# Expert pairs: the few-token way put directly behind the branch, the rare ways behind it

## The chip, the cores and the metric

The kernel runs on one core of a Trainium2 chip. The metric is the device time of one execution in microseconds. Before the change the median of three runs is 2189.8 us (2189.2 to 2190.83).

## The reference

256 tokens of width 1024 (float32 throughout) go through two networks one after the other: `first_block`, two layers with four attention branches each, and `second_block`, two layers, the first with differential attention, the second with a recurrent mixer (RWKV-7), each followed by a layer norm, a hierarchical mixture of experts and another layer norm. The change is in the mixture of experts, which is computed twice:

- A router picks for every token one of 4 groups and in it 2 of 8 experts, and gives a gate for each of the two.
- Each of the 32 experts has `w_gu` (1024 x 1024: gate and up, 512 columns each) and `w_down` (512 x 1024). For its tokens it computes `down(silu(gate) * up)`; a token's output is the gated sum over its two experts.
- 512 assignments fall on 32 experts. An expert gets 16 tokens on average, but its count depends on the data, and the kernel must be right for any count.

## The kernel before

The program is written by hand, one instruction stream for each engine, with semaphores between them (`Done` counts an engine's steps; a wait is for a count). It is fully unrolled; the only control flow are the branches spoken of here.

`sync_program` issues the weight DMAs. `experts` streams the expert weights of a stage: 16 pairs of experts, six chunks of 2 MB for each pair (`gu0` to `gu3`, `dn0`, `dn1`), into eight buffers (four of the ring, four lent from the arena). A chunk is issued once TensorE has finished with the chunk that was in its buffer eight chunks before. Nothing else moves much data in these two stages ("first stage" is the mixture of layer 0, "second stage" that of layer 1, at the end of the program).

`moe` of `tensor_program`, `vector_program` and `scalar_program` is the work on a stage. VectorE makes one-hot matrices from the routing (`places`), TensorE gathers the tokens of four experts at a time with them (`next_four` gathers for a later pair), and VectorE writes two flags for each pair: `e.flag` tells whether one of the pair's experts has more than 32 tokens, `e.flag2` whether one has more than 96. Every engine of the three loads the flags of each pair from SBUF (`value_load`) and branches. There are three ways through a pair:

- the few way (up to 32 tokens): both experts at once in column groups of 32, 32 matmuls of 512 columns for gate and up, 4 transposes, the gather for a later pair, 16 matmuls for down, 4 to bring the rows back to their tokens;
- the heavy way (33 to 96): the same for three rounds of 32 tokens, with further tokens gathered and further places turned first;
- the full way (over 96): all 256 tokens densely.

Each matmul and gather written here shows as two MATMUL and two LDWEIGHTS in the trace, being fp32, a transpose as one of each. In the order of the code a pair consists of: load of flag, branch (L910, L911 on TensorE), load of flag2, branch (L912, L913), full way, heavy way (L948 on), few way (L1032 on). So the few way is reached by jumping over the other two, the heavy way by falling through the first branch and jumping over the full way, and from the heavy way's end the code jumps over the few way (this jump is shown at L948). VectorE has its branches at L1882 and L1884, ScalarE at L2455 and L2457. All matmuls are recorded at the lines of their helpers: L410 and L417 (`mm` and `mm_to`) and L423 (`tr`).

What orders the work of a few pair on TensorE: a wait for each chunk's landing (`m.w.landed`), for ScalarE's copy of the products (`s gu`) ahead of the transposes, for VectorE's `s hs` ahead of down, and for ScalarE's `all in` of the next pair ahead of the last four matmuls. Before the first pair TensorE also waits for `first xe` (VectorE) and `0 all in` (ScalarE), two copies out of PSUM. VectorE adds a pair's product to `acc` (L1945, L1948), and behind the last pair comes the layer norm on ScalarE and VectorE.

Of the kernel before, what the change touches and what calls it, by code (L numbers as in the profile page):

```python
# [13 lines left out]
P = 128  # L14
S = 256
D = 1024
# [384 lines left out]
def tensor_program(t, m):  # L401
# [461 lines left out]
    def moe(l):  # L863
# [37 lines left out]
        for pr in range(E // 2):  # L901
# [5 lines left out]

            if pr == 0:
                t.wait_ge(*dve(M + "flags"))
            many = t.value_load(e.flag[0:1, pr:pr + 1], min_val=0, max_val=1)  # L910
            with t.If(many != 0):  # L911
                most = t.value_load(e.flag2[0:1, pr:pr + 1], min_val=0, max_val=1)  # L912
                with t.If(most != 0):  # L913

                    t.wait_ge(*dve(N + "all in"))
                    t.wait_ge(*act(N + "all in"))
                    for w in wg:
                        t.wait_ge(*m.w.landed(w))
                    for a in range(2):
                        bufs = (psum[0], psum[1]) if a else (pg, pt)  # L920
                        lst = [(dst[:, n * 256:(n + 1) * 256], gv[k // 2][:, k % 2, a * D + c * 512 + n * P:a * D + c * 512 + (n + 1) * P],
                                hT[:, k, :], k == 0, k == KT - 1)
                               for c, dst in enumerate(bufs) for n in range(4) for k in range(KT)]
                        if a:
                            mm_to(lst, before + 14, N + "gu3")
                        else:
                            mm(lst, N + "f gu0")
                    t.wait_ge(*dve(N + "f hid0"))
                    next_four(pr, pg, N + "f ")
                    for w in wd:  # L930
                        t.wait_ge(*m.w.landed(w))
                    t.wait_ge(*dve(N + "f hid1"))
                    for a in range(2):
                        h3 = e.hid[a].rearrange("p (k s) -> p k s", k=4)
                        if a:
                            t.wait_ge(*act(N1 + "all in"))
                            t.wait_ge(*dve(N + "f xe"))
                        for i in range(NT):
                            buf = (pg, pt)[i] if a else psum[i]
                            lst = [(buf[:, n * 512:(n + 1) * 512], h3[:, k, i * P:(i + 1) * P],  # L940
                                    dv[k // 2][:, k % 2, a * D + n * 512:a * D + (n + 1) * 512], k == 0, k == 3)
                                   for n in range(2) for k in range(4)]
                            if a and i:
                                mm_to(lst, before + 44, N + "out")
                            else:
                                mm(lst, N + f"f down{a}{i}")
                    t.wait_ge(*dve(N1 + "all in"))
                with t.Else():  # L948
# [80 lines left out]
                            else:  # L1029
                                mm(lst, N + "m back0")  # L1030
                    t.wait_ge(*dve(N + "m xe"))
            with t.Else():  # L1032

                pe.n = before
                xp = e.xe[pr // 2 % 2].rearrange("p (k e n) -> p k e n", k=KT, e=4)
                if pr:
                    t.wait_ge(*act(N0 + "s gu"))
                else:
                    t.wait_ge(*act(N + "all in"))
                if pr == 0:  # L1040
                    t.wait_ge(*dve(M + "first xe"))
                elif pr % 2 == 0:
                    t.wait_ge(*dve(N0 + "s xe"))
                for q in range(4):
                    t.wait_ge(*m.w.landed(wg[q]))
                    mm_to([(pg[64 * a + 32 * c:64 * a + 32 * c + 32, 0:512], xp[:, 2 * q + kk, 2 * (pr % 2) + a, :],
                            gv[q][:, kk, a * D + c * 512:a * D + (c + 1) * 512], q + kk == 0, q == 3 and kk == 1)
                           for kk in range(2) for a in range(2) for c in range(2)], before + (8, 9, 10, 14)[q], N + f"gu{q}")
                t.wait_ge(*dve(N + "all in"))
                t.wait_ge(*act(N + "s gu"))  # L1050
                tr([(psum[0][:, k * P:(k + 1) * P], e.gu[:, k * P:(k + 1) * P], idn) for k in range(4)], N + "s guT")
                next_four(pr, pt, N + "s ")
                t.wait_ge(*dve(N + "s hs"))
                for q in range(2):
                    t.wait_ge(*m.w.landed(wd[q]))
                    mm_to([(psum[0][64 * n + 32 * a:64 * n + 32 * a + 32, 512:1024], e.hs[:, 2 * q + kk, a, :],
                            dv[q][:, kk, a * D + n * 512:a * D + (n + 1) * 512], q + kk == 0, q + kk == 2)
                           for kk in range(2) for n in range(2) for a in range(2)], before + 26 + 6 * q, N + f"dn{q}")
                t.wait_ge(*act(N1 + "all in"))
                ogT = e.ogT[pr // 2 % 2][:, 256 * (pr % 2):256 * (pr % 2) + 256]  # L1060
                for i, buf in enumerate((psum[1], psum[0])):
                    lst = [(buf[:, n * 512:(n + 1) * 512], ogT[64 * n:64 * n + 64, i * P:(i + 1) * P], e.yb[64 * n:64 * n + 64, :],
                            True, True) for n in range(2)]
                    if i:
                        mm_to(lst, before + 44, N + "out")
                    else:
                        mm(lst, N + "s back0")

        ps.restart()
        ps.free = [((dve, M + "experts"), (act, M + "experts"))] * 4  # L1070
# [275 lines left out]
def vector_program(v, m):  # L1346
# [462 lines left out]
    def moe(l):  # L1809
# [35 lines left out]
        def behind_oh():  # L1845
# [2 lines left out]
            red(cnt, p[:, 64:96].rearrange("p (q a) -> p q a", a=2), MAX, M + "count")  # L1848
            ts(cnt2, cnt, 3 * CAP + 0.5, None, ALU.is_gt, None)
            cp(e.flag2, cnt2)  # L1850
            ts(cnt, cnt, CAP + 0.5, None, ALU.is_gt, None)
            cp(e.flag, cnt, M + "flags")
            gates_of(l)

# [21 lines left out]
        for pr in range(E // 2):  # L1876
            N, N1 = M + f"{pr} ", M + f"{pr + 1} "
            before = dve.n
            if pr == 0:
                v.wait_ge(*dve(M + "flags"))  # L1880
            many = v.value_load(e.flag[0:1, pr:pr + 1], min_val=0, max_val=1)
            with v.If(many != 0):  # L1882
                most = v.value_load(e.flag2[0:1, pr:pr + 1], min_val=0, max_val=1)
                with v.If(most != 0):  # L1884
                    for a in range(2):
                        bufs = (psum[0], psum[1]) if a else (pg, pt)
                        v.wait_ge(*act(N + f"f sig{a}"))
                        tt(e.hid[a], e.hid[a], bufs[0], MUL)
                        tt(e.hid[a], e.hid[a], bufs[1], MUL, N + f"f hid{a}")
# [14 lines left out]
                with v.Else():  # L1904
# [27 lines left out]
                    v.wait_ge(*pe(N + "out"))  # L1932
                    after_own()
                    v.tensor_tensor(acc[:, 1, :], acc[:, 1, :], psum[0], ADD).then_inc(*added(1, before, pr))
            with v.Else():
                dve.n = before
                g5 = psum[0][:, 0:512].rearrange("p (k a c n) -> p k a c n", k=4, a=2, c=2)
                v.wait_ge(*act(N + "s sig"))
                tt(e.sg, e.sg, g5[:, :, :, 0], MUL)
                tt(e.hs, e.sg, g5[:, :, :, 1], MUL, N + "s hs")  # L1940
                next_four(pr, pt, N + "s ")
                based(pr)
                v.wait_ge(*pe(N + "s back0"))
                after_own()
                v.tensor_tensor(acc[:, 0, :], acc[:, 0, :], psum[1], ADD).then_inc(*added(0, before, pr))  # L1945
                v.wait_ge(*pe(N + "out"))
                after_own()
                v.tensor_tensor(acc[:, 1, :], acc[:, 1, :], psum[0], ADD).then_inc(*added(1, before, pr))  # L1948
        dve.name(M + "experts")
        wide, shift = e.xe  # L1950
        for i in range(NT):
# [198 lines left out]
def scalar_program(s, m):  # L2150
# [273 lines left out]
    def moe(l):  # L2424
# [24 lines left out]
        for pr in range(E // 2):  # L2449
            N, N1 = M + f"{pr} ", M + f"{pr + 1} "  # L2450
            before = act.n
            if pr == 0:
                s.wait_ge(*dve(M + "flags"))
            many = s.value_load(e.flag[0:1, pr:pr + 1], min_val=0, max_val=1)
            with s.If(many != 0):  # L2455
                most = s.value_load(e.flag2[0:1, pr:pr + 1], min_val=0, max_val=1)
                with s.If(most != 0):  # L2457
                    for a in range(2):
                        bufs = (psum[0], psum[1]) if a else (pg, pt)
                        s.wait_ge(*pe(N + ("gu3" if a else "f gu0")))  # L2460
# [4 lines left out]
                with s.Else():  # L2465
# [17 lines left out]
                    cp(e.yb, pg[:, 0:512], N + "m yb0")  # L2483
                    s.wait_ge(*pe(N + "dn1"))
                    last(e.yb2[1], psum[0][:, 0:512], before + 15, N1 + "all in")
            with s.Else():
                act.n = before
                g5 = psum[0][:, 0:512].rearrange("p (k a c n) -> p k a c n", k=4, a=2, c=2)
                s.wait_ge(*pe(N + "gu3"))
                cp(e.gu, pg[:, 0:512], N + "s gu")  # L2490
                s.wait_ge(*pe(N + "s guT"))
                fn(e.sg, g5[:, :, :, 0], ACT.Sigmoid, N + "s sig")
                next_four(pr, pt, N + "s ")
                s.wait_ge(*pe(N + "dn1"))
                last(e.yb, psum[0][:, 512:1024], before + 15, N1 + "all in")
        act.name(M + "experts")
        for i in range(NT):

# [459 lines left out]
```

## Time and profile before

| | |
|---|---|
| median of three runs | 2189.8 us (2189.2 to 2190.83) |
| the profiled execution: its own time, its span | 2188.98 us, 2187.1 us |
| TensorE matmul / weight load, busy | 1798.6 us (82%) / 1128.6 us (52%) |
| VectorE, ScalarE, GpSimd, busy | 598.5 us (27%), 393.8 us (18%), 36.0 us (2%) |
| DMA | 539.53 MB, mean 247 GB/s |
| the chain of waits that ended last | TensorE 69%, DMA 18%, issue 5%, VectorE 5%, ScalarE 3% |

TensorE is busy for most of the span, but the shares are averages over stages with different limits. "Issue" is time in which an engine waited for nothing that the profile shows. The first mixture lies at about 885 to 1370 us of the span, the second at 1712 us to the end.

### The profile page before, as it was taken

Reading aid. Unit: us, or ns where it says so; the run is one execution under the profiler, and the core shown is the slowest. Engines: PE = TensorE matmul, PEld = TensorE weight load, DVE = VectorE, ACT = ScalarE, POOL = GpSimd, SP = SyncE. Lnnn points to the kernel's source line nnn. Section 1 sums busy time; section 2 is a strip of 40 time slices with the busy share of each in tenths; the row PEclk is TensorE's granted clock in tenths of the full one; section 3 lists DMA queues with packets and bytes.
Section 4 is the critical chain, followed back from the end, with each engine's and each line's share of the span. In section 5 each row is a group of like instructions: output and inputs, shape, how many; then the busy total and the mean of one; then the engine's idle time right before and its main releaser. Section 6 shows DMA issues by size and latency. Waiting matters only on the chain.

```text
span 2187.1 us, 30973 instructions
## 1 busy us (share of the span) xinstructions
PE 1798.6 (82%) x13574; PEld 1128.6 (52%) x13574; DVE 598.5 (27%) x1032; ACT 393.8 (18%) x760; POOL 36.0 (2%) x28
## 2 busy tenths in 40 slices
PE   6999999999999987766666878799987777876664
PEld 4788884879886764322222332575984332322211
DVE  1132312123421145221111211564345221211102
ACT  2333211313301143100000100241222010100001
POOL 0000000000000000000000000001030000000000
PEclk9999999999999998888788899899998798988977
DMA  9322333333243533899999997213004899999995
GB/s 340 97 89 97 135 137 145 141 77 135 77 154 139 207 116 150 370 425 425 425 426 425 425 400 291 77 58 117 4 23 177 365 424 426 422 425 425 425 425 224
DMA packets 51465, 539.53 MB, mean 247 GB/s; under 512 B 7440, under 2 KB 16272, under 8 KB 18224
## 3 DMA queue, kind: packets, MB, share of 16 engines
q1 hardware_dynamic: 49248, 527.06, 59.2%
q0 software_dynamic: 1152, 6.29, 0.8%
q8 instruction: 171, 2.80, 0.5%
q10 hardware_dynamic: 848, 3.00, 0.4%
q14 instruction: 46, 0.38, 0.0%
HBM read 535.28 MB, written 1.05 MB: 245 GB/s over the span
## 4 chain that ended last, share of the span: by engine, by line
PE 69%; DMA 18%; issue 5%; DVE 5%; ACT 3%; DVEq 0%; ACTq 0%
PE ps L410 53%; PE ps L417 13%; DMA arena<-in_moe_w_gu 6%; DMA ring<-in_moe_w_gu 5%; DMA arena<-in_moe_w_down 3%; DMA ring<-in_moe_w_down 3%; PE ps L423 3%; DVE x L1369 1%; ACT arena L2171 1%; DVE arena L1358 1%; ACT hb L2167 1%; DVE mT L1945 1%; DVE mT L1948 0%; ACT arena L2442 0%; ACT arena L2167 0%
## 5 line engine op out<-in xcount | busy, mean ns | idle before, releaser
L410 PE MATMUL ps<-hT,ring 128*128 128x256 f32 (+2 forms) x1888 | 391.1, 372 | 0.0
L410 PEld LDWEIGHTS ps<-hT,ring 128*128 128x128 f32 (+2 forms) x1888 | 330.7, 185 | 52.7 <-issue 3.4
L417 PE MATMUL ps<-arena 128*32 128x512 f32 (+1 forms) x1572 | 240.8, 698 | 102.6 <-issue 67.1
L417 PE MATMUL ps<-ring,arena 128*32 128x512 f32 x1472 | 213.1, 713 | 106.0 <-issue 72.5
L2171 ACT ACTIVATE arena<-ps 128x512 f32<-128x512 f32 (+4 forms) x145 | 94.5, 652 | 895.8 <-PE ps L417 519.3
L410 PE MATMUL ps<-arena 64*64 64x64 f32 (+10 forms) x1944 | 186.5, 322 | 56.3 <-ACT arena L2442 22.2
L1358 DVE TENSOR_TENSOR arena<-arena,ps 128x256 f32<-128x256 f32 (+2 forms) x82 | 46.0, 561 | 551.2 <-ACT arena L2167 464.2
L417 PEld LDWEIGHTS ps<-arena 128*32 128x32 f32 (+1 forms) x1572 | 64.5, 130 | 256.2 <-issue 202.0
L410 PEld LDWEIGHTS ps<-arena 64*64 64x64 f32 (+4 forms) x1944 | 113.8, 159 | 130.8 <-ACT arena L2442 53.4
L417 PEld LDWEIGHTS ps<-ring,arena 128*32 128x32 f32 x1472 | 53.3, 126 | 245.7 <-issue 194.4
L410 PE MATMUL ps<-ring,hT 128*128 128x256 f32 (+4 forms) x576 | 149.4, 418 | 8.7 <-ACT hT L2167 6.9
L410 PE MATMUL ps<-arena,ring 64*64 64x64 f32 (+2 forms) x1120 | 140.3, 300 | 5.9 <-DVE arena L1369 2.8
L410 PE MATMUL ps<-ring,arena 64*64 64x64 f32 (+3 forms) x1328 | 129.0, 312 | 14.1 <-issue 8.3
L410 PEld LDWEIGHTS ps<-arena,ring 64*64 64x64 f32 (+2 forms) x1120 | 122.7, 164 | 21.6 <-DVE arena L1369 3.2
L410 PEld LDWEIGHTS ps<-ring,hT 128*128 128x128 f32 x576 | 99.5, 193 | 51.0 <-issue 28.2
L410 PEld LDWEIGHTS ps<-ring,arena 64*64 64x64 f32 (+3 forms) x1328 | 72.4, 138 | 62.9 <-issue 55.9
L1945 DVE TENSOR_TENSOR mT<-mT,ps 128x1024 f32<-128x1024 f32 x29 | 35.4, 1222 | 172.7 <-PE ps L410 172.7
L423 PEld LDWEIGHTS ps<-tcom,arena 128*128 128x128 f32 (+1 forms) x370 | 41.9, 142 | 61.9 <-issue 57.6
L423 PE MATMUL ps<-tcom,arena 128*128 128x128 f32 (+1 forms) x370 | 53.4, 280 | 24.5 <-ACT arena L2171 24.5
L410 PE MATMUL ps<-ring,mT 64*64 64x64 f32 (+1 forms) x704 | 73.3, 287 | 0.2 <-issue 0.2
L2167 ACT ACT_TABLE_LOAD x50 | 64.2, 1283 | 44.6 <-DVE small L1363 18.9
L410 PE MATMUL ps<-arena,x 128*128 128x128 f32 x512 | 69.8, 296 | 1.5 <-DVE arena L1358 1.5
(173 smaller groups left out, 1259.2 us busy)
## 6 DMA issues: line engine op xcount, KB each, us to landing
ring<-in_moe_w_gu SPq DMA_DIRECT2D x64, 2048.0 KB, 28.7
arena<-in_moe_w_gu SPq DMA_DIRECT2D x64, 2048.0 KB, 31.2
arena<-in_moe_w_down SPq DMA_DIRECT2D x32, 2048.0 KB, 33.4
ring<-in_moe_w_down SPq DMA_DIRECT2D x32, 2048.0 KB, 33.4
ring<-in_w_merge SPq DMA_DIRECT2D x16, 2048.0 KB, 7.6
ring<-in_w_in SPq DMA_DIRECT2D x10, 2048.0 KB, 7.5
ring<-in_attn_w_qkv SPq DMA_DIRECT2D x6, 2048.0 KB, 7.3
ring<-in_rw_w_rkv SPq DMA_DIRECT2D x6, 2048.0 KB, 7.7
```

Source lines behind the costliest of these rows:

```text
L410: i = t.matmul(o, l, r, start=first, stop=last, skip_group_check=True)
L417: i = t.matmul(o, l, r, start=first, stop=last, skip_group_check=True)
L423: i = t.transpose(o, a, e)
L1358: v.tensor_tensor(o, a, b, op).then_inc(*dve.one(name))
L1369: v.scalar_tensor_tensor(out=o, in0=a, scalar=s, in1=b, op0=op0, op1=op1).then_inc(*dve.one(name))
L1945: v.tensor_tensor(acc[:, 0, :], acc[:, 0, :], psum[1], ADD).then_inc(*added(0, before, pr))
L2167: s.activation(o, a, f, **k).then_inc(*act.one(name))
L2171: s.activation(o, a, ACT.Copy).then_inc(*act.one(name))
```

## The change

The first flag is turned around (`few` is set where no expert of the pair has more than 32 tokens), and the two bodies of the first branch change places, on all three engines: the few way is now directly behind the branch, and the full and the heavy way, with the second flag's load and branch, are in its else part. The body of each way is the same as before. Setting the step count back (`pe.n = before`) is bookkeeping of the program that writes the code and gives no instruction. On TensorE:

```diff
-            many = t.value_load(e.flag[0:1, pr:pr + 1], min_val=0, max_val=1)
-            with t.If(many != 0):
+            few = t.value_load(e.flag[0:1, pr:pr + 1], min_val=0, max_val=1)
+            with t.If(few != 0):
+
+                pe.n = before
+                xp = e.xe[pr // 2 % 2].rearrange("p (k e n) -> p k e n", k=KT, e=4)
...
+                    if i:
+                        mm_to(lst, before + 44, N + "out")
+                    else:
+                        mm(lst, N + "s back0")
+            with t.Else():
                 most = t.value_load(e.flag2[0:1, pr:pr + 1], min_val=0, max_val=1)
                 with t.If(most != 0):
+                    pe.n = before
...
-            with t.Else():
-
-                pe.n = before
-                xp = e.xe[pr // 2 % 2].rearrange("p (k e n) -> p k e n", k=KT, e=4)
...
```

and where VectorE makes the flag:

```diff
-            ts(cnt, cnt, CAP + 0.5, None, ALU.is_gt, None)
+            ts(cnt, cnt, CAP + 0.5, None, ALU.is_lt, None)
             cp(e.flag, cnt, M + "flags")
```

VectorE's and ScalarE's streams change in the same manner. In the order of the code a pair now consists of: load of flag, branch, few way, jump over the rest, load of flag2, branch, full way, heavy way.

## Rows read from the trace of the kernel before

**Rows 1.** The page: GB/s in 40 slices; packets, MB, share of TensorE's instruction queue.

```profile
GB/s 340 97 89 97 135 137 145 141 77 135 77 154 139 207 116 150 370 425 425 425 426 425 425 400 291 77 58 117 4 23 177 365 424 426 422 425 425 425 425 224
...
q8 instruction: 171, 2.80, 0.5%
```

**Rows 2.** The chain of waits: start us, us, what.

```profile
1169.14 34.13 DMA arena<-in_moe_w_gu
...
2125.45 38.13 DMA arena<-in_moe_w_down
```

**Rows 3.** Windows: us, busy of PE, PEld, DVE, ACT, POOL; PEclk, DMA share, GB/s.

```profile
888.00:892.00 4.00, 4.00 (x28) 1.16 (x32) 0.00 (x0) 0.00 (x0) 0.00 (x0) 0.68 0.01 4
...
1716.00:1720.00 4.00, 4.00 (x24) 1.12 (x20) 0.00 (x0) 0.00 (x0) 0.00 (x0) 0.50 0.29 66
```

**Rows 4.** TensorE's branch lines: duration ns min/median/max, starts (L948: first stage alone).

```profile
L910 PEldq TENSOR_LOAD <-arena x32: 297/302/494, 881.9 to 2137.5; - x32
...
L911 PEldq COMPARE_BRANCH  x32: 80/6210/7052, 882.7 to 2138.2; - x32
...
L913 PEldq COMPARE_BRANCH  x3: 6128/6227/6317, 1217.5 to 1836.1; - x3
...
L948 PEldq COMPARE_BRANCH  x2: 313/313/313, 1267.4 to 1340.6; - x2
```

**Rows 5.** The first branch on VectorE and on ScalarE, the same columns.

```profile
L1882 DVEq COMPARE_BRANCH  x32: 50/56/72, 885.9 to 2140.7; - x32
...
L2455 ACTq COMPARE_BRANCH  x32: 40/45/55, 883.9 to 2137.4; - x32
```

**Rows 6.** TensorE in few pairs: timeline (start, us, instructions, idle before), and one branch.

```profile
911.35 5.15 PE L417 MATMUL ps<-arena 128*32 128x512 f32 x32 [5.30 <-issue]
...
928.89 1.02 PE L417 MATMUL ps<-arena 64*128 64x512 f32 x4
...
L911 PEldq COMPARE_BRANCH  x1: 6333/6333/6333, 952.0 to 952.0; - x1
...
958.52 5.43 PE L417 MATMUL ps<-ring,arena 128*32 128x512 f32 x27 [5.18 <-issue]
...
964.26 0.63 PE L417 MATMUL ps<-ring,arena 128*32 128x512 f32 x3 [0.31 <-issue]
```

**Rows 7.** Timeline at the first pair of each stage.

```profile
883.10 0.60 ACT L2171 ACTIVATE arena<-ps 128x512 f32<-128x512 f32 x1 [1.62 <-PE ps L423]
...
887.91 8.36 PE L417 MATMUL ps<-ring,arena 128*32 128x512 f32 x64 [4.84 <-issue]
...
1710.87 0.60 ACT L2171 ACTIVATE arena<-ps 128x512 f32<-128x512 f32 x1 [2.77 <-PE ps L423]
...
1714.69 1.94 PE L417 MATMUL ps<-ring,arena 128*32 128x512 f32 x8 [3.86 <-issue]
```

**Rows 8.** TensorE's timeline in pairs 12, 13 and 15 of the first stage.

```profile
1223.82 5.06 PE L410 MATMUL ps<-ring,arena 128*32 128x512 f32 x23 [5.77 <-issue]
...
1275.44 5.34 PE L417 MATMUL ps<-arena 128*32 128x512 f32 x32 [3.62 <-issue]
...
1348.82 6.56 PE L417 MATMUL ps<-ring,arena 128*32 128x512 f32 x32 [3.81 <-issue]
1355.20 3.62 PE L417 MATMUL ps<-arena 128*32 128x512 f32 x32
...
1361.64 5.28 PE L417 MATMUL ps<-arena 128*32 128x512 f32 x32 [1.39 <-DVE arena L1358]
...
1377.70 1.94 PE L423 MATMUL ps<-tcom,x 128*128 128x128 f32 x8 [8.01 <-DVE x L1369]
```

**Rows 9.** Chunks issued at 1895.2, 1718.4 and 891.2 us: time to landing.

```profile
DMA to landing us min/median/max: 11.6/11.6/11.6
...
DMA to landing us min/median/max: 7.2/7.2/7.2
...
DMA to landing us min/median/max: 7.9/7.9/7.9
```

More of the change, by code:

```diff
@@ L1031, in moe @@
                     t.wait_ge(*dve(N + "m xe"))
-            with t.Else():
-                pe.n = before
-                xp = e.xe[pr // 2 % 2].rearrange("p (k e n) -> p k e n", k=KT, e=4)
[L1036 to L1067, printed above, removed]
         ps.restart()
@@ L1880, in moe @@
                 v.wait_ge(*dve(M + "flags"))
-            many = v.value_load(e.flag[0:1, pr:pr + 1], min_val=0, max_val=1)
-            with v.If(many != 0):
+            few = v.value_load(e.flag[0:1, pr:pr + 1], min_val=0, max_val=1)
+            with v.If(few != 0):
+                dve.n = before
+                g5 = psum[0][:, 0:512].rearrange("p (k a c n) -> p k a c n", k=4, a=2, c=2)
+                v.wait_ge(*act(N + "s sig"))
+                tt(e.sg, e.sg, g5[:, :, :, 0], MUL)
+                tt(e.hs, e.sg, g5[:, :, :, 1], MUL, N + "s hs")
+                next_four(pr, pt, N + "s ")
+                based(pr)
+                v.wait_ge(*pe(N + "s back0"))
+                after_own()
+                v.tensor_tensor(acc[:, 0, :], acc[:, 0, :], psum[1], ADD).then_inc(*added(0, before, pr))
+                v.wait_ge(*pe(N + "out"))
+                after_own()
+                v.tensor_tensor(acc[:, 1, :], acc[:, 1, :], psum[0], ADD).then_inc(*added(1, before, pr))
+            with v.Else():
                 most = v.value_load(e.flag2[0:1, pr:pr + 1], min_val=0, max_val=1)
                 with v.If(most != 0):
+                    dve.n = before
                     for a in range(2):
@@ L1934, in moe @@
                     v.tensor_tensor(acc[:, 1, :], acc[:, 1, :], psum[0], ADD).then_inc(*added(1, before, pr))
[L1935 to L1948, printed above, removed]
         dve.name(M + "experts")
@@ L2453, in moe @@
                 s.wait_ge(*dve(M + "flags"))
-            many = s.value_load(e.flag[0:1, pr:pr + 1], min_val=0, max_val=1)
-            with s.If(many != 0):
+            few = s.value_load(e.flag[0:1, pr:pr + 1], min_val=0, max_val=1)
+            with s.If(few != 0):
+                act.n = before
+                g5 = psum[0][:, 0:512].rearrange("p (k a c n) -> p k a c n", k=4, a=2, c=2)
+                s.wait_ge(*pe(N + "gu3"))
+                cp(e.gu, pg[:, 0:512], N + "s gu")
+                s.wait_ge(*pe(N + "s guT"))
+                fn(e.sg, g5[:, :, :, 0], ACT.Sigmoid, N + "s sig")
+                next_four(pr, pt, N + "s ")
+                s.wait_ge(*pe(N + "dn1"))
+                last(e.yb, psum[0][:, 512:1024], before + 15, N1 + "all in")
+            with s.Else():
                 most = s.value_load(e.flag2[0:1, pr:pr + 1], min_val=0, max_val=1)
                 with s.If(most != 0):
+                    act.n = before
                     for a in range(2):
@@ L2485, in moe @@
                     last(e.yb2[1], psum[0][:, 0:512], before + 15, N1 + "all in")
[L2486 to L2495, printed above, removed]
         act.name(M + "experts")
```

28 lines of the change are left out of this document (added).

## The prediction

> **What bounds the kernel now.** I read the page first. Its row of GB/s [rows 1] has two long runs of about 425: the two expert stages, in which 192 chunks of 2 MB of expert weights come in. A pair's six chunks of 2 MB take 6 × 4.9 = 29.5 us there, and a pair that takes the way for few tokens keeps TensorE for 23.9 us: a gap of 5.3 us before 911.35 and work from there to 929.9 [rows 6], so over most of a stage TensorE has 5 to 6 us of slack per pair. The chain of waits says where that holds [rows 2]: the second stage ends on the landing of a last chunk; the first leaves the DMAs at 1203.3 and goes by TensorE to its end at 1369.7, 8.0 us before TensorE's next matmul [rows 8]. The reason is in the lines of the branches [rows 4]: of 32 pairs three take the heavy way (the branch for the full way is always taken, so none needs that). By their times they are pairs 12 and 14 of the first stage and pair 5 of the second. A heavy pair holds TensorE for some 50 us against 29.5 us of stream, so with two among the last four pairs the stage ends on TensorE. The stream is stopped in one more place, each stage's start: all eight buffers are full until the first pair frees one, and 888 to 892 and 1716 to 1720 us show 4 and 66 GB/s [rows 3].
>
> Then the branches. The flag takes 0.30 us to load [rows 4] and, with two register steps, 0.65 us until its branch. The branch behind it takes 0.08 us where it is not taken and some 6.2 us where it is taken to the few code, over the full and the heavy code [rows 4]. It is no slow instruction: the heavy pairs' branch over the full code alone takes 6.2 us too, while the jump from the end of the heavy code over the few code takes 0.31 us. Counted in the code, with two matmuls and two weight loads in the trace for each fp32 matmul written, the few code is some 250 instructions, the heavy one 750, the full one 680.
>
> How much is there behind a landing? The branch at 952.0 ends at 958.35; 27 matmuls follow, and the next waits until 964.26 [rows 6], 5.9 us after the landing. I read this as one block present and the following one usable 5.9 us later.
>
> **The change, part by part.** It swaps which way falls through. Nothing is computed otherwise, and no DMA is moved.
>
> 1. *Few to few (24 of 30 passages).* Before: load 0.65, taken branch 6.2. After: a jump of 6.2 at the end of the few code, over heavy and full code, then load 0.65 and 0.08. The same work, in another order, in the same gap of 5.3 us [rows 6]: 0, and where the stream bounds there are 6 us of cover besides. ScalarE and VectorE take their branches in 0.04 to 0.07 us, over the same distance [rows 5]: 0.
>
> 2. *The first pair of a stage.* Nothing is jumped over. TensorE must still wait for the copies of ScalarE, over at 883.70 and 1711.47 [rows 7]; with 0.15 us behind them its matmuls start at 883.85 instead of 887.91 and 1711.65 instead of 1714.69: -4.1 and -3.0. Besides, the granted clock was 0.68 and 0.50 of full speed behind these gaps [rows 3], so at the lower level, 1.2 GHz, for most or all of the stretch. With a gap of 0.8 us I expect the higher level, 2.4 GHz, to stay. The first 64 matmuls of the first stage took 8.4 us [rows 7] against twice 3.6, 32 of a later pair 5.3 against 3.6 [rows 8]: the first buffer comes free 1.1 to 1.7 us sooner, and I take 1.4. The stream, idle here, moves with it: -5.4 and -4.4. The last pair's new jump lies beside the layer norm, in TensorE's 8.0 us idle [rows 8] in the first stage and behind its last work in the second: 0; without that cover it would cost its 6.3.
>
> 3. *Few to heavy (3).* Before, from load to first matmul 7.7 us in pair 12 (the load starts at 1216.1, as the last matmuls of pair 11 do, the heavy ones at 1223.8, [rows 8]). After: jump 6.3, load 0.65, a taken branch over the few code, whose target is in the block that comes 5.9 us after the landing (so 5.25 more), load 0.65, branch over the full code 6.9 (behind the block just asked for, as the longest of the row that reaches 7.05), 0.1. Sum 19.8: +12.1. The lowest bound for the middle branch is the 0.31 us of the jump over the same code [rows 4], the highest a wholly new fetch, 6.9.
>
> The Trainium skill, "Runtime: NRT & Kernel Launch", Instruction fetch mechanics, gives TensorE 128 KiB of code memory, 2048 instructions, and also says that prefetch is sequential over a two-page window. By the first figure a branch over 250 instructions would always land in loaded code; by the second it waits as in my sum. The jumps of some 1,430 and 680 instructions that take 6.2 us speak for the second.
>
> 4. *Heavy to few (3).* The heavy code is now the last and falls through. Before, TensorE idled 3.6 to 3.8 us here (its queue still ran while the sequencer fetched) and restarted at the lower level: the first 32 matmuls took 5.3 us in pair 13 and 6.56 in pair 15, against 3.6 at the higher [rows 8]. After: -3.6 and -1.6 at pair 13; -3.8 and -2.9 at pair 15, and -1.6 for its last 32 (5.28 us), if the clock stays up.
>
> *First stage.* Pair 12 still begins on a landed chunk, so it moves with the stream, and from there all is TensorE: -5.4 + 12.1 - 3.6 - 1.6 + 12.1 - 3.8 - 2.9 - 1.6 = +5.3.
>
> *Second stage.* Its end moves with the stream: -4.4, plus what heavy pair 5 takes from it. TensorE comes out of pair 5 later by 12.1 - 3.7 = 8.4. The tightest chunk is issued at 1895.2 and lands 11.6 us later, where an idle stream needs 7.2 to 7.9 [rows 9]: 4.1 of slack. The rest, 4.3, the stream loses. Net -0.1.
>
> Sum +5.2. The profiled execution took 2188.98 us (span 2187.1, 1.9 around it), so 2194.2 by its own time; it stands 0.8 below the median of 2189.8, which gives the forecast, 2195.0. Its own range is 2190 to 2200: 1.65 us twice for the middle branch at its upper bound, 1 to 2 us for what a heavy pair's start costs at the lower clock after a longer gap, and as much the other way. A measurement tells 0.2% from no change here, 4.4 us; this case lies just above that.
>
> **Rivals.** *The middle branch is cheap* (faster). If TensorE's memory reaches 250 instructions past a landing at once, few to heavy costs 6.3 + 0.65 + 0.31 + 0.65 + 6.9 + 0.1 = 14.9, +7.2 instead of +12.1. First stage -4.5; in the second, 12.1 becomes 7.2 and the stream's slack holds it, -4.4. That is 8.9 less than 2189.8: 2180.9. It decides once the wait in that branch is under about 3 us. For it: 0.31 us for the same distance. Against: there the engine had long read ahead, and the stall at 964.26. The page's first figure (the Trainium skill, as above) would give this case.
>
> *The clock does not come back* (slower). Nothing in rows shows what is granted to these stretches when the gap before them goes. Without the gains of 1.4 + 1.4 + 1.6 + 2.9 + 1.6: +8.9 on the forecast, 2203.9; a tenth of it already puts the time over the bound of 0.2%. For it: pair 15 is slow even in its last 32 matmuls, far from the gap. Against: matmuls behind gaps of 0.8 us keep their 3.6.
>
> *The change does not reach the order of code.* If the compiler lays the blocks out by its own mind, nothing moves: 2189.8. Against: 0.08 and 6.2 us follow the order in the source.
>
> **Chances.** Forecast 0.55, cheap branch 0.20, no clock gain 0.17, no change 0.08. Of the forecast about 0.23 is within 0.2% and 0.32 above. Faster is the cheap branch, 0.20; within 0.23 + 0.08 = 0.31; slower 0.32 + 0.17 = 0.49. The range runs from just above the middle of the cheap case to just beyond the clock case, 2182 to 2205; that leaves out about 0.11 below and 0.07 above.
>
> **What would show it.** Step 1: the branch behind the flag at 0.08 us for few pairs, a jump of some 6.2 us at the end of their code, gaps of 5.3 us unchanged. Step 2: first matmul 0.8 us behind the gather's last, no hole of 7 us in the stream. Step 3: on three pairs a taken branch behind the flag of about 5.3 us (0.31 decides for the first rival), and a gap of 18 us before the heavy matmuls. Step 4: no gap behind heavy pairs. The stream between pairs 5 and 6 of the second stage pauses for some 4 us. The forecast is wrong if the first stage ends earlier than before against its start, or if few pairs in midstream make the stream pause.

## The result, and the profile after

| | before | after |
|---|---|---|
| median of the runs made side by side | 2189.5 us (6 runs, 2183.7 to 2194.6) | 2198.6 us (6 runs, 2195.9 to 2201.0) |
| the profiled execution: its own time, its span | 2188.98, 2187.1 us | 2200.56, 2198.8 us |

The changed kernel takes 1.0042 of the time before (95%: 1.0031 to 1.0053), 9 us more. The forecast was 2195.0 us, slower, range 2182 to 2205: the sign came and so did the mechanism at the heavy pairs; the loss is larger than the +5.2 of the forecast.

The branches come first, as they decide between forecast and first rival. The rows are TensorE's branch instructions after the change, a row for each window that I asked for (duration in ns min/median/max, then the starts). L911 holds the branch behind the flag and the jump at the end of the few way, L949 the branch over the full way.

```profile
L911 PEldq COMPARE_BRANCH  x61: 73/3594/6761, 884.9 to 2179.6; - x61
...
L911 PEldq COMPARE_BRANCH  x1: 6119/6119/6119, 1215.9 to 1215.9; - x1
L911 PEldq COMPARE_BRANCH  x2: 5401/5760/6119, 1215.9 to 1222.8; - x2
L911 PEldq COMPARE_BRANCH  x1: 5797/5797/5797, 1306.4 to 1306.4; - x1
L911 PEldq COMPARE_BRANCH  x1: 5382/5382/5382, 1850.2 to 1850.2; - x1
...
L949 PEldq COMPARE_BRANCH  x3: 6732/6987/7372, 1228.9 to 1856.3; - x3
```

61 branches at L911 are 32 at the flag and 29 at the end of few ways. Against [rows 4]: the branch at the flag takes 0.07 to 0.09 us where it is not taken, and that is now the case that leads to the few way; the jump at the end of the few way takes some 6.2 us (6.12 in the row at 1215.9). In front of each of the three heavy pairs the middle branch takes 5.40, 5.80 and 5.38 us (forecast 5.25, rival 0.31), and the one over the full way 6.7 to 7.4 us (forecast 6.9).

The start of a stage, from the timeline (start us, us, engine, line, what, idle before), and the windows (busy us of PE, PEld, DVE, ACT, POOL; PEclk; DMA share; GB/s), to be held against [rows 7] and [rows 3]:

```profile
885.73 0.60 ACT L2174 ACTIVATE arena<-ps 128x512 f32<-128x512 f32 x1 [1.74 <-PE ps L423]
886.38 7.07 PE L417 MATMUL ps<-ring,arena 128*32 128x512 f32 x64 [0.69 <-ACT arena L2174]
...
908.80 3.64 PE L417 MATMUL ps<-arena 128*32 128x512 f32 x16 [5.56 <-issue]
```

```profile
886.00:890.00 4.00, 3.62 (x36) 1.20 (x40) 1.64 (x6) 0.33 (x1) 0.00 (x0) 1.00 0.59 205
1726.00:1730.00 4.00, 4.00 (x40) 1.04 (x32) 0.00 (x0) 0.00 (x0) 0.00 (x0) 1.00 1.03 373
```

The idle time before the first matmul of the stage is 0.69 us instead of 4.84, the first 64 matmuls take 7.07 us instead of 8.36, and the granted clock is full. The gap between the first two few pairs is 5.56 us, where it was 5.30 [rows 6].

TensorE's timeline in pairs 12 to 15, against [rows 8]:

```profile
1211.91 3.22 PE L417 MATMUL ps<-arena 128*32 128x512 f32 x16 [3.19 <-DMA arena<-in_moe_w_down]
1215.90 1.13 PE L410 MATMUL ps<-arena 64*128 64x512 f32 x4 [0.77 <-ACT arena L2445]
...
1236.03 5.30 PE L410 MATMUL ps<-ring,arena 128*32 128x512 f32 x19 [18.14 <-issue]
...
1284.16 3.64 PE L417 MATMUL ps<-arena 128*32 128x512 f32 x32
...
1299.23 1.13 PE L410 MATMUL ps<-arena 64*128 64x512 f32 x4 [0.77 <-ACT arena L2445]
...
1320.42 1.93 PE L410 MATMUL ps<-arena 128*32 128x512 f32 x6 [19.20 <-issue]
1323.44 5.45 PE L410 MATMUL ps<-arena 128*32 128x512 f32 x26 [1.09 <-issue]
...
1352.60 1.92 PE L410 MATMUL ps<-ring,arena 128*32 128x512 f32 x16 [0.74 <-DVE arena L1359]
...
1368.39 3.64 PE L417 MATMUL ps<-ring,arena 128*32 128x512 f32 x32
...
1378.29 5.34 PE L417 MATMUL ps<-arena 128*32 128x512 f32 x32 [1.39 <-DVE arena L1359]
1384.40 1.13 PE L410 MATMUL ps<-arena 64*128 64x512 f32 x4 [0.77 <-ACT arena L2445]
...
1394.39 1.94 PE L423 MATMUL ps<-tcom,x 128*128 128x128 f32 x8 [8.00 <-DVE x L1370]
```

Two idle stretches of 18.14 and 19.20 us stand before the heavy pairs (5.77 before pair 12 in the old kernel), and none behind them. The windows, columns as above, show the granted clock: half of full speed as the heavy matmuls of pairs 12 and 14 start, and full in the few ways of pairs 13 and 15 up to 1377 us.

```profile
1236.00:1240.00 4.00, 3.97 (x18) 1.06 (x19) 0.00 (x0) 0.00 (x0) 0.00 (x0) 0.50 0.99 418
1284.00:1288.00 4.00, 4.00 (x38) 1.19 (x40) 1.22 (x1) 0.00 (x0) 0.00 (x0) 1.00 0.60 205
1320.00:1324.00 4.00, 2.48 (x10) 0.42 (x14) 0.00 (x0) 0.00 (x0) 0.00 (x0) 0.50 0.04 12
1324.00:1328.00 4.00, 4.00 (x25) 1.20 (x18) 0.00 (x0) 0.00 (x0) 0.00 (x0) 0.60 0.02 4
1212.00:1215.00 3.00, 3.00 (x16) 0.50 (x16) 0.00 (x0) 0.00 (x0) 0.00 (x0) 0.57 1.00 426
1373.00:1377.00 4.00, 3.09 (x28) 0.94 (x20) 0.00 (x0) 0.66 (x2) 0.53 (x1) 1.00 0.99 368
1379.00:1383.00 4.00, 4.00 (x28) 1.13 (x24) 1.72 (x2) 0.00 (x0) 0.00 (x0) 0.65 0.26 81
```

In the new profile's chain these two stretches, and the one before heavy pair 5 of the second stage, are now links of their own (start us, us, what):

```profile
1222.22 13.80 issue
...
1305.59 14.83 issue
...
1845.56 17.66 issue
```

And the page's GB/s in 40 slices:

```profile
GB/s 339 98 86 96 134 144 136 140 77 134 79 151 162 182 115 170 406 424 425 426 424 425 377 380 249 94 39 154 4 23 144 412 425 424 367 426 425 424 424 247
```

Against [rows 1], the stages start with 406 and 412 in place of 370 and 365, and slice 35 has 367: behind heavy pair 5 of the second stage the stream now loses time.

### The profile page after: what moved, and what is told of

The parts are those of the page before. It is cut to its first block, busy times and chain, and to the rows that moved or that the text cites. A ratio compares the mean times of both kernels' runs of the same rounds, so it can differ in the third digit from the quotient of the medians.

```text
span 2198.8 us, 31054 instructions
## 1 busy us (share of the span) xinstructions
PE 1790.1 (81%) x13574; PEld 1121.2 (51%) x13574; DVE 598.6 (27%) x1032; ACT 393.8 (18%) x760; POOL 36.0 (2%) x28
## 4 chain that ended last, share of the span: by engine, by line
PE 68%; DMA 18%; issue 6%; DVE 4%; ACT 3%; DVEq 0%; ACTq 0%
PE ps L410 53%; PE ps L417 13%; DMA arena<-in_moe_w_down 5%; DMA arena<-in_moe_w_gu 5%; DMA ring<-in_moe_w_gu 4%; DMA ring<-in_moe_w_down 3%; PE ps L423 3%; ACT arena L2174 1%; DVE x L1370 1%; DVE arena L1359 1%; ACT hb L2170 1%; DVE mT L1893 1%; ACT arena L2445 0%; ACT arena L2170 0%; DVE mT L1896 0%
## 5 line engine op out<-in xcount | busy, mean ns | idle before, releaser
L417 PE MATMUL ps<-ring,arena 128*32 128x512 f32 x1472 | 204.5, 690 | 91.2 <-issue 68.0
L2170 ACT ACT_TABLE_LOAD x50 | 64.2, 1283 | 44.6 <-DVE small L1364 18.9
## 6 DMA issues: line engine op xcount, KB each, us to landing
ring<-in_moe_w_down SPq DMA_DIRECT2D x32, 2048.0 KB, 26.9
```

The lines of the kernel that those rows point to most:

```text
L417: i = t.matmul(o, l, r, start=first, stop=last, skip_group_check=True)
L2170: s.activation(o, a, f, **k).then_inc(*act.one(name))
```

## The experiments

In most of these kernels the two bodies behind the flag are wrapped in two local functions, unchanged (`few_way`, and `rare_ways` with the second flag), and each pair chooses an order:

```diff
+            if cond:                      # new order
+                with t.If(many == 0):
+                    few_way()
+                with t.Else():
+                    rare_ways()
+            else:                         # old order
+                with t.If(many != 0):
+                    rare_ways()
+                with t.Else():
+                    few_way()
```

An experiment is then a `cond` for each engine. Two columns of the table come from the profile: the first stage's tail, from the last four matmuls of pair 11 to those of pair 15; and the second stage's stream, from its eighth chunk's landing to its last chunk's.

| kernel | median us | ratio to before (95%) | tail | second stream |
|---|---|---|---|---|
| c1_old_again | 2188.3 | 0.9995 (0.9985 to 1.0006) | 151.1 | 450.5 |
| c1_new_again | 2199.3 | 1.0051 (1.0034 to 1.0068) | 168.4 | 447.7 |
| c1_pe_only | 2197.0 | 1.0046 (1.0032 to 1.0061) | 166.0 | 451.5 |
| c3_others_only | 2190.6 | 1.0001 (0.9987 to 1.0014) | 149.9 | 449.3 |
| c1_first_pair | 2183.7 | 0.9982 (0.9971 to 0.9993) | 148.4 | 448.2 |
| c2_first_three | 2184.5 | 0.9972 (0.9957 to 0.9987) | 151.4 | 447.2 |
| c3_late_new | 2201.4 | 1.0053 (1.0037 to 1.0069) | 165.4 | 450.3 |
| c2_allfew_old | 2162.4 | 0.9873 (0.9853 to 0.9893) | 124.4 | 449.0 |
| c2_allfew_new | 2154.8 | 0.9841 (0.9821 to 0.9861) | 123.0 | 444.1 |
| c2_new_heavy_first | 2189.8 | 1.0003 (0.9991 to 1.0015) | 158.6 | 448.5 |
| c3_first3_rare_swapped | 2179.1 | 0.9949 (0.9930 to 0.9968) | 148.0 | 444.1 |

In the profiles of `before` and `after` the tails are 151.6 and 168.5 us. One profile stands behind each number of these two columns: where TensorE's code in the tail is that of the old kernel, five profiles give 148.4 to 151.6 us, so differences of up to 3 us between two tails say nothing. The second stream of the same kernel differs by 0.9 us (`before`, `c1_old_again`) and by 1.9 us (`after`, `c1_new_again`).

**The two kernels again** (`c1_old_again`, `c1_new_again`; no edit).

> The kernel before, unchanged, to see how its time and its single stages vary from one execution to the next. Both theories: 2189.5 us within 2 us, ratio 1.000. In its profile the first mixture (from TensorE's load of the first flag to the load of the first flag of the second mixture) took 826.3 us in the first profile and 837.2 us with the change, of which 3.7 us were gained in the stretch between the mixtures, where nothing was changed: if that is the chip's own variation, this profile shows the stretch from 1367.7 to 1708.1 us (340.4 us) shorter or longer by 2 us or more.

> The kernel with the change once more. Theory (code blocks: the stream starts 4.7 and 5.4 us sooner, each passage from a few pair to a heavy pair costs 12 to 13 us more, each passage back is 1 to 3.5 us shorter): 2197 to 2199 us, ratio 1.003 to 1.005, and in the profile again 5.3 to 5.9 us in the branch behind the flag of the three heavy pairs. Rival (the difference is chance between executions): ratio 1.000 to 1.002.

The old kernel gave 0.9995, the new one 1.0051: the loss repeats, and so do its branches. The stretch between the stages that the first expectation names took 337.4 us here after 340.4 in `before`, so 3.0 us less in the same kernel. This row is its middle branch before pair 12 (the other two took 5.58 and 4.90 us):

```profile
L911 PEldq COMPARE_BRANCH  x1: 5325/5325/5325, 1222.0 to 1222.0; - x1
```

**Which engine** (`cond` true on TensorE alone; on VectorE and ScalarE alone).

> The new order on TensorE alone; VectorE and ScalarE keep the old one. Theory (all of the change is TensorE's fetching of code): as with the whole change, 2197 to 2199 us. Rival (the jumps of VectorE and ScalarE at the end of the few way, in front of their next step, carry part of it): 2192 to 2195 us.

> The new order on VectorE and ScalarE alone, the old one on TensorE. Theory (all of the change is TensorE's code): as before the change, 2189 us, ratio 0.999 to 1.001. Rival (their jumps behind the few way delay the copies and sums that TensorE waits for): above 2191 us.

TensorE alone gives 1.0046, the other two 1.0001 (0.9987 to 1.0014). So the loss lies in TensorE's order of code, and what the other two engines add is below the 3 us that this run can tell.

**The start alone** (TensorE: `cond = pr == 0`, then `pr < 3`).

> The old order everywhere except in the first pair of each mixture on TensorE, where the few way comes directly behind the branch. Its end then has a jump and the next pair a taken branch, some 13 us between pairs 0 and 1 once, in a stretch where the weights stream is ahead. Theory (gain at the start of the stream, loss at the heavy pairs): only the gain is left, 4.7 and 5.4 us, so 2179.5 us, ratio 0.995. Rival (the start gives nothing that lasts, the stream's pause is only moved): 2189 us. Second rival (the double jump between pairs 0 and 1 takes the gain back): 2186 to 2193 us.

> The new order on TensorE in pairs 0 to 2 of each mixture, the old one in the rest. In the run with pair 0 alone the double passage (a jump, then a taken branch, 13 us) stood between pairs 0 and 1, where a chunk's buffer came free only 8.2 us ahead of its landing, and the streams kept 3.2 us of their 4.8. Here it stands between pairs 2 and 3, where there are over 12 us. Theory: the streams keep 4.8 and 5, the time falls by 3 us more, 2179 to 2181 us, ratio 0.996. Rival (the double passage was harmless, and the gain is what it is): 2183.7 us as before.

With pair 0 alone turned round the time falls to 0.9982, under both kernels, but 4 us above the 2179.5 that I had expected. The price of the seam, the place where the order changes, is in the timeline: TensorE jumps away at the end of pair 0's few way and again, in the old order, at pair 1's flag, and idles 12.37 us once.

```profile
887.04 7.07 PE L417 MATMUL ps<-ring,arena 128*32 128x512 f32 x64 [0.69 <-ACT arena L2198]
...
916.27 1.08 PE L417 MATMUL ps<-arena 128*32 128x512 f32 x4 [12.37 <-issue]
```

Counted from the eighth chunk's landing, the first stage's stream is 4.6 us ahead of `before` at the last chunk of pair 1 and 3.2 us ahead at that of pair 2; in the second stage it is 4.8 and 2.7 us. Three pairs in the new order move the seam to where the stream should have slack. I had expected some 3 to 5 us more from it; its time, 2184.5 us, is that of the rival, and its ratio of 0.9972 is not told apart from 0.9982. Where the seam lies, in front of pair 1 or of pair 3, is then worth less than these runs can tell.

**The late pairs alone** (TensorE: `cond = pr >= 11`; no gain at the start, both heavy pairs of the first stage's end in the new order, pair 5 of the second stage in the old).

> The new order on TensorE only from pair 11 of each mixture on, so without the sooner start of the streams, and with heavy pairs 12 and 14 of the first mixture behind it; heavy pair 5 of the second keeps the old order. Theory (gain and loss are separate and add up): the first mixture's stream starts as before, and its end comes some 18 us later than before (13.8 us with the change, and the 4.8 of the start missing); the second mixture is as before; 2205 to 2209 us. Rival (gain and loss hang together, so that without the sooner start the heavy pairs cost less): 2202 us or less.

1.0053, as slow as the whole change, though it leaves the second stage alone. The tail is 14.3 us longer than that of `c1_old_again`, against 17.3 for the whole change. The idle stretches before the heavy pairs are nearly the same:

```profile
1238.11 4.36 PE L410 MATMUL ps<-ring,arena 128*32 128x512 f32 x24 [18.05 <-issue]
1243.81 1.06 PE L410 MATMUL ps<-ring,arena 128*32 128x512 f32 x8 [1.33 <-issue]
...
1320.86 7.10 PE L410 MATMUL ps<-arena 128*32 128x512 f32 x32 [18.45 <-issue]
```

Together with the first-pair kernel this shows the two parts, each by itself: the start alone wins some 4 us of time, the late pairs alone lose 11 us of it, and 14 us in the profile's tail. That the two simply add up is not shown. The median of 2201.4 us lies 4 us below my interval and meets the rival's 2202 or less, while the profiled execution was the slowest of the eight (2204.5 us).

**No heavy pair at all** (the flag is set over 1000 tokens instead of 32, in the old and in the new order). These two leave out the tokens of an expert beyond its first 32, so that no pair leaves the few way; their difference is all that the change does without rare ways.

```diff
-            ts(cnt, cnt, CAP + 0.5, None, ALU.is_gt, None)
+            ts(cnt, cnt, 1000.0, None, ALU.is_gt, None)
```

> The old order, with the first flag's threshold raised so that no pair takes the heavy way: the three heavy pairs are computed for the first 32 tokens of each expert alone, and the rest of their tokens is left out. No passage to or from heavy code is left. Theory: both mixtures are bound by the weights stream to their ends; the first mixture's end then follows the stream (last chunk some 5 x 4.9 us before TensorE's end no longer), so the time is below that of the kernel before by what TensorE overran in the first mixture: 2168 to 2178 us.

> The new order with the same raised threshold (the same tokens of the three heavy pairs left out). Theory: without heavy pairs only the sooner start of the two streams is left of the change, so 4.7 + 5.4, some 10 us less than the run with the old order and the same threshold. Rival (the start's gain does not last to the end of the program): equal to it within 2 us. Second rival (few to few costs something too in the new order): more than it.

The old order took less than I had expected by some 6 us: three heavy pairs cost 27 us of the time before. Between the two orders lie 7.5 us in favour of the new one (2162.4 to 2154.8); I had expected 10. In the profiles the two streams are shorter by 4.1 and 4.9 us. In the GB/s rows of the two, old first, the starts of the streams differ, 370 to 401 and 365 to 407, and behind them both keep 423 to 426 to the last slices of a stage. The jump at the end of each few way costs no stream.

```profile
GB/s 343 98 90 98 136 136 144 147 78 102 113 119 172 180 112 110 370 423 425 426 425 425 425 424 398 85 78 80 4 39 198 365 424 425 425 425 426 426 424 223
```

```profile
GB/s 341 98 96 98 137 137 144 138 89 98 118 118 176 176 118 81 401 424 425 424 426 426 425 425 401 105 55 103 4 28 195 407 424 424 425 425 425 425 425 221
```

**The heavy way ahead of the full way** (new order, and `most` turned round, so that the heavy way follows the few way at once and the full way is last; on all three engines).

```diff
-                with t.If(most != 0):      # full
-                ...
-                with t.Else():             # heavy
+                with t.If(most == 0):      # heavy
+                ...
+                with t.Else():             # full
```

> The new order with the two rare ways exchanged: few, heavy, full. The branch over the full code (7 us) falls away in front of heavy code, and behind heavy code comes a jump over the full code (some 6.2 us, of which 3.6 lie beside TensorE's queue). Theory: the gap from few to heavy shrinks from 20 us between the matmuls' starts to 13, that behind heavy pairs grows from nothing to 3.4 us and brings back the lower clock there (1.6 and 2.9 us): 2 to 4 us below the kernel with the change, 2194 to 2197 us. In the profile the middle branch still takes 5 to 6 us, since the code that it goes to is as far behind its landing as before. Rival (what is long in front of heavy code is the heavy way's own wait and not the fetch): the gap stays at 18 us.

2189.8 us, 1.0003, better than I had expected. The second branch now falls through, the gap before the heavy matmuls shrinks from 18.14 to 11.33 us, and the jump comes back at the heavy way's end:

```profile
L951 PEldq COMPARE_BRANCH  x1: 6035/6035/6035, 1267.5 to 1267.5; - x1
```

```profile
1226.14 5.23 PE L410 MATMUL ps<-ring,arena 128*32 128x512 f32 x32 [11.33 <-issue]
...
1274.48 2.78 PE L417 MATMUL ps<-arena 128*32 128x512 f32 x22 [2.56 <-issue]
1279.34 1.56 PE L417 MATMUL ps<-arena 128*32 128x512 f32 x9 [2.09 <-issue]
```

The 6.0 us jump shows as 2.56 us idle, as TensorE still worked on queued matmuls after the jump had begun. The 2.09 us end 5.8 us after the jump does, so they fit the wait for the following block of code that the prediction reads out of [rows 6]. So the third branch's 7 us count in full in front of a heavy pair, and a jump behind it counts for less.

**The best of both** (TensorE: new order for `pr < 3`, old order behind that; and on all three engines, in all pairs, the heavy way ahead of the full one. A pair from 3 on is then laid out as heavy, full, few).

> As the run with the new order in pairs 0 to 2 alone, and in every pair of TensorE the heavy way ahead of the full one. A heavy pair of the old order is then reached with two branches that are not taken (about 0.8 us of fetch and load in place of 7.0), but its end jumps over the full and the few code, 930 instructions, where it jumped over 250. Theory: in front of a heavy pair 6.2 us fall away and the clock stays up (1.5 us); behind it come 6.2 us more before the load and the next taken branch, of which nothing is covered: zero to 2 us less for each heavy pair, the first mixture's end 0 to 4 us sooner than in the run with pairs 0 to 2 alone, 2179 to 2184 us. Rival (the jump from the end of the heavy code goes to the few way's own closing point in two steps, each fetched): 5 us more for each heavy pair, 2190 us or more.

2179.1 us, 0.9949 (0.9930 to 0.9968), the fastest of the kernels that compute all tokens, and below both. How much of that the exchange of heavy and full way gave is not shown: the interval overlaps that of `c2_first_three` (0.9957 to 0.9987), and of the 3.4 us between their two tails 1.6 lie in pair 15's last 32 matmuls, which differ by as much between kernels with the same code there (see step 4 below). A heavy pair is now reached with no jump at all. It pays behind: the first row is the jump at the heavy way's end, the second the next pair's branch to its few code, and the timeline shows the 9.80 us idle that the two leave.

```profile
L951 PEldq COMPARE_BRANCH  x1: 6157/6157/6157, 1258.2 to 1258.2; - x1
...
L1078 PEldq COMPARE_BRANCH  x1: 7196/7196/7196, 1265.0 to 1265.0; - x1
```

```profile
1272.41 6.04 PE L417 MATMUL ps<-arena 128*32 128x512 f32 x32 [9.80 <-issue]
```

## Why the prediction was right, and where its sizes were off

**What bounds the kernel** held: the first stage ends on TensorE, the second on the stream. `c2_allfew_new` shows the one, as without heavy pairs the first stage's tail is stream again, 123 us; the GB/s rows show the other.

**Step 1, few to few, 0**: right. TensorE's idle stretches of this kind have a median of 5.0 us before and 5.2 us after, `c2_allfew_new` keeps 423 to 426 GB/s through the passages of a stage, and `c3_others_only` gives VectorE's and ScalarE's part as nothing that can be measured.

**Step 2, the first pair**: right at the start, too large at pair 12. Matmuls start 0.69 us behind what frees them, at the higher clock, and in the first stage the time from the eighth chunk's landing to pair 1's last chunk's falls from 26.9 to 22.0 us, -4.8 for -5.4; in the second stage it falls by 5.4, for -4.4. The clock came back in both stages, 1.00 in the windows above for 0.68 and 0.50 in [rows 3]. But pair 11's last four matmuls come only 2.3 us sooner against the stream's start, 3.1 short: the stream is 5.0 us ahead at pair 10's last chunk and 3.3 at pair 11's, and pair 11's last 16 matmuls wait for their chunk and go mostly at the lower clock (3.22 us, 0.57 of full speed at 1212 to 1215 us). The step "it moves with the stream" took the start's gain for the gain ten pairs later. A part of the 3.1 us is chance: in `c1_old_again`, the same kernel as `before`, pair 11's last chunk lands 2 us later against the stream's start than in `before`, and from `c1_old_again` to `c1_new_again` the matmuls come 3.8 us sooner, so 1.6 short. The jump at the end of the stage's last pair costs nothing, as forecast: TensorE is idle for 8.00 us there, after 8.01 [rows 8].

**Step 3, few to heavy, +12.1 each**: the mechanism is shown, each term by its row. From the start of the last four matmuls to the heavy way's first, 7.7 us and 7.9 us became 20.1 and 21.2 (1236.03 less 1215.90; 1320.42 less 1299.23), +12.4 and +13.3, 1.5 us more than the two terms. The middle branch was 5.40 and 5.80 us for 5.25. The first rival asked for 0.31 and under 3: it is ruled out by all fourteen such branches of the five kernels that have them (`after`, `c1_new_again`, `c1_pe_only`, `c2_new_heavy_first`, `c3_late_new`), 4.86 to 5.80 us. `c2_new_heavy_first` takes the 6.7 to 7.4 us of the third branch away and gets 6.8 us of the gap before pair 12 back.

The Trainium skill, "Advanced Engine Details and Errata", ISA Cache, says that a line of the code cache is 16 KB, 256 instructions, and that there are only 2 of them. The trace agrees in the size, 16.4 KB a packet [rows 1], and a branch over 250 instructions that takes 4.86 to 5.80 us fits the number. The same list gives TensorE 128 KB, which would hold the whole few way and more; nothing in these rows bears that out.

**Step 4, heavy to few**: the gaps went, the clock came back only in part. Pair 12's heavy matmuls to pair 13's first: 51.6 to 48.1 us, -3.5 for -3.6. Pair 13's few way: 16.8 to 15.1, -1.7 for -1.6. Pair 14's to 15's: -0.7 where I had -3.8. This is the term that failed most, by 3.1, and it fails in the kernels run again too (-0.1). The sum took the heavy pair itself as unchanged. Behind 19.20 us of idleness its first 32 matmuls need 8.40 us until the next group starts (6 in 1.93 us, a new idle stretch of 1.09, 26 in 5.45), where they needed 5.25 behind 5.95 us of idleness:

```profile
1300.13 5.32 PE L410 MATMUL ps<-arena 128*32 128x512 f32 x32 [5.95 <-issue]
```

That row is from `before`. The other kernels fit: the same 32 took 4.07 us in `c3_first3_rare_swapped`, which has no such gap, 5.70 in `c2_new_heavy_first` behind 10.64 us, and 7.0 to 9.0 us in the four kernels with a gap of 17.8 to 19.2 us. So what the missing gap behind the heavy pair won was given back at its start.

Pair 15: its first matmuls are at the higher clock again and the few way shrinks from 18.9 to 16.0 us, but its last 32 stay at 5.34 us (0.65 at 1379 to 1383 us) where I had given -1.6. The pair gave -2.9 for -4.5. These last 32 do not follow the order of the code: with the old order in the tail they took 5.25 to 5.28 us in three profiles and 3.64 in two. This row is from `c3_others_only`, where TensorE has the old order throughout:

```profile
1365.10 3.64 PE L417 MATMUL ps<-arena 128*32 128x512 f32 x32 [1.39 <-DVE arena L1371]
```

What decides between the two is open. So a part of the second rival, that the clock does not come back, came after all: behind a longer gap a heavy pair starts at the lower level and pays there what is saved behind it.

The table has the first stage's terms, each as after less before: in the profiles of `before` and `after`, and in those of `c1_old_again` and `c1_new_again`, the repeat (us; the sums are those of unrounded values).

| term | forecast | first profiles | repeat |
|---|---|---|---|
| stream's start to pair 11's last four matmuls | -5.4 | -2.3 | -3.8 |
| from there to pair 12's first | +12.1 | +12.4 | +12.3 |
| to pair 13's first | -3.6 | -3.5 | -2.9 |
| pair 13's few way | -1.6 | -1.7 | -1.7 |
| from there to pair 14's first | +12.1 | +13.3 | +12.6 |
| to pair 15's first | -3.8 | -0.7 | -0.1 |
| pair 15's few way | -4.5 | -2.9 | -2.8 |
| first stage | +5.3 | +14.6 | +13.5 |

**Second stage, -0.1**: right in the net, with both parts about a microsecond larger than forecast. From the eighth chunk to the last the stream takes 449.6 us after 449.7: it gains 5.4 at the start and loses 5.5 behind heavy pair 5 (3.6 and 6.7, against `before`, in `c1_new_again` and `c1_pe_only`; `c1_new_again` less `c1_old_again` gives a net of -2.8), where a chunk issued at 1899.0 meets an idle queue and lands in 7.1 us. [rows 9] had 11.6 us there.

```profile
DMA to landing us min/median/max: 7.1/7.1/7.1
```

```profile
1908.00:1912.00 4.00, 4.00 (x35) 1.20 (x35) 1.37 (x2) 0.00 (x0) 0.00 (x0) 1.00 0.63 264
```

The sum of the two profiles: before the first mixture +2.1 (the same instructions; it varies from one execution to the next), first stage +14.6, between the stages -3.5, second stage -0.1, behind the last chunk -1.5 (the last 16 matmuls are at the higher clock), in all +11.6 of the 11.7 us between the spans. By the medians it is +9. The -3.5 between the stages, in code that the change does not touch, had no step in my sum, and these profiles do not show that the change made it. The expectation of `c1_old_again` had set the test for the chip's own variation, 2 us or more in the same kernel, and 3.0 us came. From pair 15's last four matmuls to the second stage's eighth chunk the two profiles of the old kernel have 346.2 and 343.3 us, the two of the new one 342.7 and 340.8, and all kernels of the table together 341 to 350. Nor did the -1.5 behind the last chunk come back at the same place: in `c1_new_again` these 16 matmuls took 3.64 us.

So the direction and the two stages' roles were foreseen, but that the time lies within 4 us of the forecast is in part luck. The first stage alone missed by 9.3 us (8.2 in the repeat), and the two terms of -3.5 and -1.5, which the sum did not have, gave back 5 of them. Against `after`, the tail of `c3_late_new` is 3.1 us shorter: 2.3 of it are in the first 32 matmuls of the two heavy pairs (6.69 and 7.03 us against 7.59 and 8.40), 0.8 in the passage to pair 14. What made them faster is open.

One remark in the prediction does not follow from its numbers: a tenth of the lost clock gain is not needed to pass the bound of 0.2%, 2194.2 us, as the forecast of 2195.0 is already above it.

**The last rival**, that the order in the source does not reach the chip, is ruled out by the branch rows.

## What to carry to other kernels

A branch in an unrolled program is priced by where its target lies in the code, so lay out first what is reached without cover: here the heavy passages at the end of a stage bound by TensorE, and the first pair of a stage, while the 24 common passages cost the same in either order. The rule to put the common case behind the branch lost 9 us here, because it set two more fetches, one after the other, in front of the rare case, and the rare case was the critical one. Each place can have its own order: three pairs turned round and the heavy way put ahead of the full one together gave 10.9 us (2190.0 to 2179.1, side by side).

## What the runs showed that I had not expected

- A branch over only 250 instructions, taken right after code has been jumped to, is not cheap: 4.9 to 5.8 us in fourteen rows, nearly the price of a far jump (median 6.2 us, mostly 5.7 to 6.8; less at the end of a stage's last pair, 3.5 and 3.6 us). Over about the same code it takes 0.31 us at the end of a heavy way [rows 4]. Far jumps that follow close on another taken branch took more, 6.7 to 7.4 us, as in all three rows of L949 and at L1078.
- A jump of 6.1 us idles TensorE by very different amounts: 5.56 us between few pairs, 2.56 us behind a heavy way that ends in it, 18.14 us where three branches follow one another.
- A gap costs more than its length. The first 32 matmuls of pair 14 took 4.07 us with no gap before them, 4.9 to 5.6 behind 6 us, 5.70 behind 10.64 us and 7.0 to 9.0 behind 17.8 to 19.2 us. The few ways behind the heavy pairs, whose gaps the change took away, start at 3.64 us for 32 instead of 5.3 and 6.56 [rows 8].
- Two profiles of the same code place the same work differently by 2 to 3 us: pair 11's last chunk by 2 us, the stretch between the stages by 3.0 us, and pair 15's last 32 matmuls take 3.64 or 5.3 us in kernels with the same code there. A term of that size needs more than one pair of profiles.
